# Attention of the two layers in sixteen rounds of four units, where it ran in thirty-two steps of two

## The reference, cut to what matters

```
h = rmsnorm(x) ; p = split(h @ w_in)                 # 512 x 1024 times 1024 x 19 slices
o_a = mla(...)          # branch A: 4 heads, keys of 64 + 32 columns (rope)
o_b = diff_attn(...)    # branch B: 4 heads, each with TWO softmax maps of 32 columns; a = p0 - lam * p1
o_c = dsa(...)          # branch C: 4 heads of 64 columns, only the top 128 keys of each query count
o_d = short_conv(...)   # branch D
x = x + concat(o_a*silu(g), o_b*silu(g), o_c*silu(g), o_d*silu(g)) @ w_out
```

## Time and profile before

| what | us |
|---|---|
| median of 3 runs | 1785.37 |
| lowest and highest | 1785.29 and 1786.74 |
| the profiled execution, its span | 1785.4 |
| TensorE busy in it | 1776.4 |
| VectorE busy | 1062.3 |
| ScalarE busy | 750.5 |
| GpSimd busy | 407.3 |

### The profile page before, as it was taken

The page is one execution under the profiler, slowest core; times in us unless marked ns, Lnnn a source line. Parts: engine busy times, 40 slices in busy tenths (PEclk is TensorE's granted clock), DMA queues, the critical chain, the costliest instruction groups (busy, mean ns, idle before and its releaser), DMA issues.

```text
span 1785.4 us, 25187 instructions
## 1 busy us (share of the span) xinstructions
PE 1776.4 (99%) x9274; PEld 1437.2 (80%) x9274; DVE 1062.3 (59%) x2106; ACT 750.5 (42%) x1386; POOL 407.3 (23%) x248
## 2 busy tenths in 40 slices
PE   9999999999999999999999999999999999999998
PEld 7767778776777888888888878879888888888887
DVE  5888777588877665445433445555756654555333
ACT  6464654446454533223222455545444322232222
POOL 4544553455354310000000232220200200000000
PEclk9999999999999999999999999999999999999999
DMA  5422222322212343333333422323321333333332
GB/s 188 125 81 70 60 59 85 97 81 83 67 53 60 96 138 102 95 94 94 106 106 104 150 60 83 95 72 107 95 73 55 92 101 94 94 94 101 99 106 94
DMA packets 49765, 165.53 MB, mean 93 GB/s; under 512 B 5640, under 2 KB 6152, under 8 KB 49672
## 3 DMA queue, kind: packets, MB, share of 16 engines
q1 hardware_dynamic: 48376, 161.47, 30.2%
q10 hardware_dynamic: 1296, 2.84, 0.4%
HBM read 162.12 MB, written 2.17 MB: 92 GB/s over the span
## 4 chain that ended last, share of the span: by engine, by line
PE 97%; DVE 1%; ACT 1%; issue 0%; POOL 0%; DVEq 0%; POOLq 0%
PE proj L1013 78%; PE turned L1302 2%; PE o L1326 2%; PE score L1276 2%; PE turned L1530 1%; PE proj L1460 1%; PE o L1556 1%; PE score L1521 1%; PE proj L1453 1%; PE score L1285 1%; PE o L1652 1%; PE turned L979 1%; PE score L1641 1%; PE score L1163 0%; PE proj L991 0%; PE turned L998 0%
## 5 line engine op out<-in xcount | busy, mean ns | idle before, releaser
L1013 PE MATMUL proj<-hhi,whi 128*128 128x512 f32 x1456 | 580.2, 399 | 0.6 <-DVE tanh L2285 0.3
L1013 PE MATMUL proj<-hhi,wlo 128*128 128x512 f32 x1456 | 568.1, 390 | 0.0
L1013 PE MATMUL proj<-hlo,whi 128*128 128x512 f32 x1456 | 567.3, 390 | 0.0
L1736 ACT ACTIVATE whi<-ring 128x1024 fp32r<-128x1024 f32 x279 | 295.2, 1058 | 622.7 <-PE proj L1013 614.4
L2201 DVE TENSOR_TENSOR wlo<-ring,whi 128x1024 fp32r<-128x1024 f32 x199 | 243.1, 1222 | 164.8 <-ACT whi L1736 164.5
L1013 PEld LDWEIGHTS proj<-hhi,whi 128*128 128x128 f32 x1456 | 274.3, 188 | 59.4 <-issue 6.6
L1013 PEld LDWEIGHTS proj<-hhi,wlo 128*128 128x128 f32 x1456 | 273.4, 188 | 58.8
L1013 PEld LDWEIGHTS proj<-hlo,whi 128*128 128x128 f32 x1456 | 274.0, 188 | 52.8
L759 POOL TENSOR_TENSOR wlo<-ring,whi 128x1024 fp32r<-128x1024 f32 x80 | 194.7, 2435 | 372.6 <-ACT whi L1736 372.0
L771 POOL TENSOR_TENSOR prob<-prob 128x512 f32<-128x512 f32 x36 | 56.6, 1574 | 873.9 <-ACT prob L1732 873.9
L1762 ACT ACTIVATE prob<-prob,negmax 128x256 f32<-128x256 f32 (+3 forms) x208 | 114.4, 552 | 65.5 <-DVE negmax L2274 64.1
(11 more groups left out here) (334 smaller groups left out, 2426.1 us busy)
## 6 DMA issues: line engine op xcount, KB each, us to landing
ring<-wstream SPq DMA_DIRECT2D x287, 512.0 KB, 3.6
arena<-lines SPq DMA_DIRECT2D x28, 256.0 KB, 5.5
arena<-x ACTq DMA_DIRECT2D x4, 512.0 KB, 5.9
out<-arena SPq DMA_DIRECT2D x8, 256.0 KB, 2.9
arena<-mem SPq DMA_DIRECT2D x1, 1024.0 KB, 9.4
ring<-wstream ACTq DMA_DIRECT2D x2, 256.0 KB, 7.3
arena<-hot SPq DMA_DIRECT2D x2, 80.0 KB
par<-params ACTq DMA_DIRECT2D x2, 74.0 KB, 1.9
```

Of the source, the lines that this page charges most:

```text
L1013: mm = pe.matmul(b, rounded(w), rounded(rhs(v, k)), start=(first and n == 0 and p == 0), stop=(last and n == len(blocks) - 1 and p == 2))
L1736: act.activation(rounded(dst), src, ACT.Copy, scale=scale).then_inc(ready, 1)
```

## The change

Steps are joined in pairs to rounds `t` of 0 to 15, four units each. The four units of a round use four banks, `four_banks = (score[0], score[1], turned[0], turned[1])`, both for the scores and for the transposed maps. In B the four units of a round are the two maps of two heads, with `u` innermost in the loop, so the four matmuls of one part stand on the four row groups. The order on TensorE in a round is: the transposes of round t - 1, the fillers of slot 2t, the scores of round t, the products with V of round t - 1, the fillers of slot 2t + 1. Slot 2t is dealt 2.4 (in the plan's units, in which a chunk is 0.68), the rest goes to the odd slots. Because scores and transposes share banks, `scores(t)` waits for ScalarE's copies of all maps of round t - 1 (`turn_out`), and in a layer's first round for `latent_ready`. VectorE and ScalarE are written out again by rounds. The places of the evictions of o move with them (`O_ROUND`).

```diff
+def round_need(t):
+
+    if t == ROUNDS:
+        return 4.5
+    return 3.8 + 0.85 * step_qb(2 * t) if 2 * t < B_STEPS else 5.5
...
-            pieces.append((name, 0, {"UQ": 2.9, "UK": 1.5, "UV": 1.5, "VN": 0.5, "SS": 1.0, "SR": 1.0}[name[:2]]))
+            pieces.append((name, 0, {"UQ": 2.0, "UK": 1.0, "UV": 1.1, "VN": 0.45, "SS": 1.7, "SR": 1.6}[name[:2]]))
...
+        four_banks = (score[0], score[1], turned[0], turned[1])
...
-                def scores(s):
-
-                    if s == 0:
+                def scores(t):
+
+                    if t == 0:
                         pe.wait_ge(relu_ready, L * IDX_UNITS + IDX_UNITS)
+                        pe.wait_ge(latent_ready, L * 3 + 3)
                         pe.wait_ge(b_ready, L * 4 + 2)
                     else:
-                        pe.wait_ge(min_ready, L * LAYER_SM + 2 * s)
+                        pe.wait_ge(min_ready, L * LAYER_SM + 4 * t)
+                        pe.wait_ge(turn_out, L * LAYER_GR + groups_before(2 * t))
...
+                    elif branch == "B":
+                        for p, (q_part, k_part) in enumerate(((bq_hi, bk_hi), (bq_hi, bk_lo), (bq_lo, bk_hi))):
+                            for u in range(4):
+                                part(u, q_part, k_part, p == 0, p == 2)
...
-                for s in range(FILL_STEPS + 1):
-                    if s < STEPS:
-                        scores(s)
-                    if s >= 3:
-                        pv(s - 3)
-                    if 2 <= s < FILL_STEPS:
-                        turn(s - 2)
-                    for name, k in PLAN[s] if s < FILL_STEPS else ():
+                for t in range(ROUNDS + 1):
+                    if t == 0:
+                        scores(0)
+                    else:
+                        turn(t - 1)
+                    for name, k in PLAN[2 * t]:
+                        fill(name, k)
+                    if 0 < t < ROUNDS:
+                        scores(t)
+                    if t > 0:
+                        pv(t - 1)
+                    for name, k in PLAN[2 * t + 1]:
                         fill(name, k)
...
+                for t in range(LAST_STEP // 2 + 1):
+                    a, b = 2 * t, 2 * t + 1
+                    y_lows(a)
+                    gates_of(a - 2)
+                    topk_of(a)
+                    convs_of(a - 1)
+                    for name in ENDED[a] if t <= ROUNDS else ():
+                        evict(name)
+                    if t < ROUNDS:
+                        row_mins(t)
...
+                    if t < ROUNDS:
+                        row_scales(a)
+                        row_scales(b)
```

More of the change, by code:

```diff
@@ L217 @@
 FILL_STEPS = STEPS + 2
+ROUNDS = STEPS // 2
 QB_ORDER = (0, 3, 1, 2)
+FIRST_PART = 2.4
 def step_qb(s):
@@ L1279, in parts @@
                             mm.then_inc(score_done, 1)
-                    branch, pair, qb = UNITS[2 * s][:3]
+                    branch = UNITS[4 * t][0]
                     if branch == "A":
-                        for b in range(2):
-                            hh, q, W = 2 * pair + b, slice(qb * P, (qb + 1) * P), width(qb)
-                            pe.matmul(score[b][:, 0:W], qA[0:96, hh, q], kA[0:96, hh, 0:W], start=True, stop=True).then_inc(score_done, 1)
-                    else:
[L1287 to L1290, removed]
@@ L1314, in pv @@
+                def pv(t):
+                    branch, pair = UNITS[4 * t][:2]
+                    o = step_groups(2 * t)[0] // 8
+                    if groups_before(2 * t) % 8 == 0:
                         if o >= 2:
@@ new lines, in gates_of, with diags_of, y_highs @@
+                def gates_of(s):
+                    for name in ENDED[s] if 0 <= s < FILL_STEPS else ():
+                        if name[:2] == "GT":
+                            gate(int(name[2]))
+                def diags_of(s):
+                    if 1 <= s - END["SS0"] <= 2:
+                        subln_diag(s - END["SS0"] - 1)
+                def y_highs(s):
+                    for c in Y_ORDER:
+                        if Y_HIGH[c] == s:
+                            high_y(c)
+                for t in range(LAST_STEP // 2):
+                    if 0 < t <= ROUNDS:
+                        copy_groups(t - 1)
+                    gates_of(2 * t - 1)
+                    after_slot(2 * t)
+                    diags_of(2 * t)
+                    y_highs(2 * t)
+                    if t < ROUNDS:
+                        for u in range(4):
+                            a = 4 * t + u
+                            s = a // 2
+                            softmax_exp(L * LAYER_SM + (a + 1), u, width(step_qb(s)),
+                                        first_sum(s) if s < B_STEPS and u % 2 == 0 else None)
+                    gates_of(2 * t)
+                    if t == SQUARE_ROUND:
```

223 lines of the change are left out of this document (107 added, 116 removed).

## The result

The changed kernel takes 1808.58 us (median of 4 runs, 1808.16 to 1810.89) against 1785.33 (1785.01 to 1786.74) for the kernel before: a ratio of 1.0129, with a 95% interval of 1.0116 to 1.0142. Forecast were 1785.6 us, from 1776 to 1799. The profiled execution's span is 1807.1 us, against 1785.4 before, so 21.7 us are to be explained. Wherever both figures are on record, the time of an execution is about 1.8 us above its span (1808.86 and 1807.1 here). So the span of 1785.4 belongs to an execution of about 1787.2 us and not, as was said ahead of the prediction, to one at the median. Its trace has one stretch of TensorE at half speed in the layers, which costs 1.7 us; that executions near the median lack it would explain why the medians are 23.2 us apart and the spans 21.7, but no trace of such an execution shows it.

What follows compares the result with a forecast made beforehand. TensorE, busy 99% of the span, was taken as the bound. 1785.4 - 18.6 (leaving TensorE) + 9.6 (layer starts) + 6.0 (B's second pair) + 1.0 (SR0) + 1.6 (C's end) + 0.6 (clock) = 1785.6 us, range 1776 to 1799.

Steps and rivals of the forecast that it cites:

- leaving TensorE: TensorE's own work in the layers falls by 18.6 us (17.6 to 19.5): row groups 12.0, switches 6.1, B rounds 0.5.
- round 0's transposes: Each layer's first transposes wait for VectorE's scalings behind two search halves, one held by GpSimd: 3.4 and 2.2 us.
- B's second pair: DB0 waits 2.8 us for GpSimd's low part, or transposes wait for VectorE; together 3.0 per layer, 6.0 us.
- round of SR0: Its first part holds only the spread, too short to cover ScalarE's copies: 0.5 us per layer, 1.0 (0 to 2.5).
- C: transposes of rounds 13 and 15: At C's end VectorE has 8 to 9 us between two rounds of minima: 0.8 per layer, 1.6 (0 to 4).
- clock: Term in the sum: new waits and joined transposes may bring one more half-speed stretch of TensorE, 0.6 us.
- switches of configuration: TensorE changes matmul configuration less often in A's and C's rounds, 0.09 us a switch: 6.1 us saved.
- The limit it feared at width 128: B scores: loads of 128 columns going one by one would keep up to half of 0.47 us per round.
- The start of a layer: New TensorE waits at `scores(0)`, round 0's transposes and `scores(1)` in both layers: 9.6 us (8.2 to 12).
- the rival's mechanism: Clock rival: each TensorE wait of 2 us or more drops the clock, four drops of 1.8: 1792 us, chance 0.07.
- VectorE becomes the bound: VectorE's work lies between scores and transposes: 1795.6 us, chance 0.20; mark: L2500 and like waits in A alone over 15.
- The gain stays: VectorE and GpSimd hold up TensorE only at the start of the layers: 1776.4 us, chance 0.28.

Runs made afterwards that it cites:

- Number 10: Number 9 with the products with V of the round before placed between B's two pairs of maps (rounds 1 to 7): 1779.5 us.
- number 3: The changed kernel with VectorE scaling each round's two maps before the early evictions, in place of behind them: 1793.6 us.
- number 4: The changed kernel with GpSimd's low parts due in a round's second part held until that round's scalings are done, VectorE's order left: 1794.7 us.
- number 9: The changed kernel with number 3's edit, query turns moved on GpSimd, round 0 and 2 orders mended, two BQ1 chunks ahead of `scores(0)`: 1776.2 us, ratio 0.9944 to the kernel before.
- number 6: The changed kernel with most of the search left out (halves from the fourth on work on 8 columns), for timing alone: 1804.5 us.
- numbers 7: The changed kernel with number 3's edit and A's query turns two slots earlier on GpSimd: 1781.3 us, ratio 0.9974 to the kernel before.
- number 5: The changed kernel with B's scores written in pairs of maps again, all else left: 1809.0 us.

## Why the prediction was wrong, by its own steps

| term, us | on record | measured |
|---|---|---|
| leaving TensorE | -18.6 | -18.3 |
| latents at `scores(0)` | 2.0 | 2.0 |
| round 0's transposes | 5.6 | 4.9 |
| `scores(1)` for the copies | 2.0 | 0.8 |
| B's second pair: DB0, and transposes of round 6 | 6.0 | 9.7 + 4.3 |
| `scores(3)` for the copies | 0 | 3.0 |
| A: transposes of rounds 8 and 10 | 0 | 4.3 |
| round of SR0 | 1.0 | 0 |
| C: transposes of rounds 13 and 15 | 1.6 | 6.4 |
| clock | 0.6 | 4.5 |

**What leaves TensorE: right**, in sum and in its largest part. Number 10 gives 9.9 for the row groups, where the record had 10.5 for them in 16 rounds and number 10 undoes 14. The share of the switches of configuration, 6.1 on record, was not measured by itself. The limit it feared at width 128 isn't there: twelve of these take 0.48 (74.79 to 75.27), as six did.

**The start of a layer: right in sum** (9.6 on record, 7.7), with every wait at the line that was named.

**The step that failed most is the scaling.** Its held form was read off and priced once, for round 0. The step "In all other rounds of A and C it has four chunks, 2.7, and the copies are covered" looked at what follows the transposes and never at what comes before them. The order on VectorE, an early eviction and then both scalings, was in the diff, and so was the other half of the collision, that the end of the same job starts the low part. Pricing each round's held scaling would have given up to 2 us in five rounds of a layer, less the cover there. Measured: 4.3 in round 6, 4.3 in A and 6.4 in C, 15.0 us, against 1.6 and a share of the 6.0. Numbers 3 and 4 take 15.0 and 15.3 us of waits away, from two sides.

**DB0's wait: right mechanism, too small a size.** TensorE came 21.5 us after GT0's end, as on record (118.5 to 140.0). GpSimd took 26.2 (to 144.7) against 24.3: four of its twelve turn operations, beside VectorE's work, ran 1.6 to 1.8 us in place of 1.28. The hold can stretch GpSimd's rows as it does VectorE's, and I took the unheld row. Nor did one wait hide the other: DB0's came ahead of round 6, and that round's transposes waited as well.

**`scores(3)` was not priced.** Round 2 ends three up-projection jobs at once. ScalarE has six copies (0.59 each) and two splits (1.04 and 1.06) between the exponentials and the copies of the maps; the second split alone ends at 109.91, when TensorE has been ready since about 109.7.

**The clock: the rival's mechanism happened inside the main course.** I gave it 7% as a case of its own, but for the most part it is a consequence of waits: stretches at 1.2 GHz came 0.3 and 0.75 us after the waits of 4.85, 0.6 after one of 2.4, and after two of 1.4 and 0.8 in a row in the second layer, not after the same two in the first. In number 9, with no wait over 1.8, there was none. Beside such waits it belongs in the sum, at 1.7 us for a stretch of 3.4. It isn't tied to waits alone: in the kernel before, and once in number 4, a stretch came with no wait near, 3.4 and 3.5 us after the start of the sum SS0, sixteen matmuls of two columns. TensorE before its one drop in the layers, at 208.75:

```profile
205.38 1.84 PE L979 MATMUL proj<-halves,arena 128*128 128x2 f32 x16
207.08 1.54 PE L1285 MATMUL score<-arena 96*128 96x384 f32 x4
```

**The rivals.** "VectorE becomes the bound" had its sign right. Its own mark, over 15 us, was reached only if C's rounds count (L2500 and L2506 together 17.3, without C 11.5), and its reason was wrong: number 6 takes the load away and leaves the waits. It was queue order and the hold between VectorE and GpSimd. "The gain stays" is what numbers 7 and 9 show to have been possible. The range ended at 1799 because the rivals were priced apart, though a late scaling, a late low part and the clock all come together when the lag is halved.

What stays open: why the clock fell behind the two short waits in one layer and not in the other, and after SS0 in some executions and not in others.

## What to carry to other kernels

When a change shortens the lag between a producer and the engine that bounds the kernel, go through every round and list what stands ahead of the producer's operation in its queue, and what other engine is started by the same event; the stretched rows that the old lag hid are in the old trace, seven in a layer here. Then mend the orders before judging the change: two edits of order turned +1.3% into -0.3%, and five into -0.6%. And when the bound engine has been made faster, expect the next one in line to take its share, as waits, over half of them for GpSimd, took two thirds of the row groups' gain.

## What the runs showed of the hardware that I had not expected

- Matmuls on different row groups start out of program order: in number 5 the seventh of twelve started 0.02 us after the first, ahead of the third (0.33 later), and all twelve took 0.91 us. With the products with V between the pairs, in number 10, they did not run beside each other. The Trainium skill, "TensorE: Matmul & The Clock Gate", section "Step-by-step: what each phase is for", says that matmuls stay in program order and only weight loads are pulled ahead; this trace differs.
- The hold between VectorE and GpSimd works both ways and on small operations: an operation of 32 rows in a `q_rope` took 1.6 to 1.8 us beside VectorE's operations in four cases of twelve, and 1.27 to 1.29 in the others.
- A wait of TensorE of 4.85 us brought a stretch at half the clock each time it occurred. In the changed kernel and in number 5 it was 3.4 us long, from 0.2 us before the work came back to 0.75 after, and cost about 1.7 us. In both layers of number 3 it was 6.8 us long and began inside the wait (142.69, where the work came back at 145.22).
